# A fused two-block transformer kernel on one core: later slots for the layer work beside the expert gathers, another order of jobs in the tail

## The reference, cut to what matters

```python
# first block, its last part
ids, gates = top16 of two 128-way scores, per head     # 8 heads x 16 = 128 rows per token
ub = take(u_tab, ids); a = einsum('td,ted->te', h, ub)
w = gates * gelu(a)
vb = take(v_tab, ids); y = einsum('te,ted->td', w, vb)
x = rmsnorm(x + g2 * y, final_g)

# second block, two layers
for l in range(2):
    z = rmsnorm(x) @ w_in[l]         # g_q, g_k, g_v, g_lr, g_gate, c_q, c_kv, k_pe, m_gate
    o_gla = rms(gated_linear_attention(g_q, g_k, g_v, decay(g_lr))) * silu(g_gate)
    q, k, v = low-rank projections of rms(c_q), rms(c_kv), with head norms and rope
    o_mla = causal_softmax_attention(q, k, v) * silu(m_gate)
    x = x + concat(o_gla, o_mla) @ w_out[l]
```

## Time and profile before

| | us |
|---|---|
| median of three runs | 1138.64 |
| profiled execution | 1140.25 |
| its span | 1138.4 |
| PE / VectorE / ScalarE / GpSimd busy | 990.1 / 655.7 / 325.2 / 521.2 |
| chain that ended last: PE / DMA / GpSimd | 51% / 23% / 9% |

### The profile page before, as it was taken

The page is one execution under the profiler, slowest core; times in us unless marked ns, Lnnn a source line. Parts: engine busy times, 40 slices in busy tenths (PEclk is TensorE's granted clock), DMA queues, the critical chain, the costliest instruction groups (busy, mean ns, idle before and its releaser), DMA issues.

```text
span 1138.4 us, 11282 instructions
## 1 busy us (share of the span) xinstructions
PE 990.1 (87%) x3307; PEld 535.2 (47%) x3307; DVE 655.7 (58%) x1543; ACT 325.2 (29%) x813; POOL 521.2 (46%) x575
## 2 busy tenths in 40 slices
PE   3999999999997868878679899879889987987986
PEld 3868656855452323323235344335345333643653
DVE  5866776985755756856574774566554544142132
ACT  4123232222212111110144543233623211440441
POOL 1210011767777777777566456655554760000000
PEclk9999999999999998989989999999998988998999
DMA  9998955999999999999999999999997999548440
GB/s 341 321 391 308 337 205 170 385 376 408 409 410 412 410 413 413 411 412 402 408 410 409 406 410 399 406 405 409 408 410 279 400 409 389 212 162 282 162 148 19
DMA packets 142041, 394.92 MB, mean 347 GB/s; under 512 B 16744, under 2 KB 23456, under 8 KB 141856
## 3 DMA queue, kind: packets, MB, share of 16 engines
q0 software_dynamic: 75392, 274.86, 61.5%
q1 hardware_dynamic: 64224, 118.61, 28.7%
q10 hardware_dynamic: 2368, 0.76, 0.3%
HBM read 393.15 MB, written 1.05 MB: 346 GB/s over the span
## 4 chain that ended last, share of the span: by engine, by line
PE 51%; DMA 23%; POOL 9%; issue 7%; DVE 5%; ACT 4%; POOLq 0%; DVEq 0%; SPq 0%; ACTq 0%
PE bank L1720 16%; DMA wring<-in_peer_u,ids 14%; PE bank L1768 11%; PE bank L1454 8%; POOL wring L979 5%; DMA R<-in_w_in 3%; DMA wring<-in_peer_v,ids 3%; PE bank L1789 3%; PE bank L1531 2%; PE bank L1444 2%; DMA R<-in_peer_u,ids 2%; POOL R L979 2%; DVE R L1991 1%; DVE wring L2332 1%; ACT R L1292 1%
## 5 line engine op out<-in xcount | busy, mean ns | idle before, releaser
L2332 DVE CUSTOM_DVE_ANT_0 wring<-wring,bank 128x1024 f32<-128x1024 f32 x224 | 272.8, 1219 | 206.7 <-DMA wring<-in_peer_u,ids 203.4
L979 POOL DMA_INDIRECT wring<-in_peer_v,ids x224 | 214.1, 956 | 168.3 <-PE bank L1720 98.3
L1720 PE MATMUL bank<-wring,R 128*128 128x512 f32 x496 | 239.4, 628 | 32.8 <-ACT R L1218 23.1
L979 POOL DMA_INDIRECT wring<-in_peer_u,ids x224 | 211.4, 944 | 76.0 <-issue 56.4
L1720 PE MATMUL bank<-wring,modb 128*128 128x512 f32 x384 | 184.6, 621 | 25.1 <-ACT modb L1218 17.8
L1720 PEld LDWEIGHTS bank<-wring,R 128*128 128x128 f32 x496 | 95.9, 200 | 161.2 <-issue 130.1
L1720 PEld LDWEIGHTS bank<-wring,modb 128*128 128x128 f32 x384 | 72.2, 197 | 114.3 <-issue 95.9
L1018 POOL TENSOR_SCALAR small<-small 128x1 f32<-128x1 f32 (+3 forms) x15 | 2.9, 192 | 254.2 <-ACTq L1299 144.9
L1768 PE MATMUL bank<-R,hT 128*128 128x512 f32 (+1 forms) x192 | 94.5, 623 | 13.5 <-issue 6.8
L1768 PE MATMUL bank<-wring,hT 128*128 128x512 f32 (+1 forms) x192 | 88.6, 613 | 4.3 <-ACT hT L1399 2.7
L1454 PE MATMUL bank<-hT,wring 128*128 128x256 f32 x304 | 70.9, 392 | 1.8 <-DVE hT L2015 1.0
(11 more groups left out here) (374 smaller groups left out, 1248.7 us busy)
## 6 DMA issues: line engine op xcount, KB each, us to landing
wring<-in_w_in SPq DMA_DIRECT2D x14, 2048.0 KB, 14.5
wring<-in_ada_w SPq DMA_DIRECT2D x8, 2048.0 KB, 13.9
R<-in_w_in SPq DMA_DIRECT2D x8, 2048.0 KB, 21.1
wring<-in_w_out SPq DMA_DIRECT2D x6, 2048.0 KB, 10.8
wring<-in_ada_w SPq DMA_DIRECT2D x8, 1024.0 KB, 15.3
R<-in_w_out SPq DMA_DIRECT2D x4, 2048.0 KB, 20.3
wring<-in_peer_wq SPq DMA_DIRECT2D x2, 2048.0 KB, 10.2
wring<-in_peer_u,ids POOLq DMA_INDIRECT x224, 12.1
```

What stands on the lines that cost most here:

```text
L979: pool.indirect_dma_start(dst, None, table, bass.IndirectOffsetOnAxis(index, 0)).then_inc(landed, 16)
L1720: last = pe.matmul(pb[half][:, :], diag[b][:, s, :], v_place(n, b, s)[:, half * 512:(half + 1) * 512], start=False, stop=last_row, skip_gr ...
L2332: dve.tensor_tensor_reduce(row, row, h_psum(t), 1.0, 0.0, ALU.mult, ALU.add, a8[:, b, s:s + 1]).then_inc(u_free, 1)
```

## The change

`VISIT` goes from 52 to 59, so that visit 1 starts at slot 75 and not 68, and the last job in the shadow lies in slot 126, not 112. Within a visit, most jobs that read another engine's result move to one or two slots behind it. The three orders in the tail change: two of the eight pieces of `y2` of visit 1 and one `y2e` move to the beginning of visit 3; `mg` 0 and 1 move ahead of `qkt`, and `gge` behind `qkte`; `ms` 1, `mPT`, `go` and `gosq` move forward, `mPT` 2 and 3 with their evacuation go ahead of `goe`. SyncE starts chunk 6 of layer 1 four products earlier, and stores tile 0 of the output at the very end of its list.

```diff
-VISIT = 52
+VISIT = 59
@@ visit_slots
-    at(13, ("gqk", 2))
-    at(14, ("gqk", 3))
-    at(15, ("gqke",), ("gl",))
-    at(16, ("gate",), ("u", 0))
...
-    at(18, ("decays",), ("u", 1))
-    at(20, ("gv", 0), ("glaq",))
...
-    at(28, ("gg", 3), ("qkt",))
-    at(29, ("gge",), ("qkte",), ("go",))
-    at(30, ("mg", 0), ("gosq",))
...
+    at(14, ("gqk", 3))
+    at(15, ("cT",))
+    at(16, ("cTe",), ("gqke",))
+    at(17, ("gl",))
+    at(18, ("gate",), ("u", 0))
+    at(20, ("u", 1))
+    at(21, ("decays",), ("ue", 1), ("gv", 0))
...
+    at(25, ("gve",), ("gg", 0), ("keT",))
+    at(26, ("keR",), ("rope", 2), ("gg", 1), ("A",))
+    at(28, ("Am",), ("gg", 3), ("U",))
+    at(29, ("gge",), ("st",))
+    at(30, ("qkt",))
+    at(31, ("qkte",))
+    at(32, ("go",), ("mg", 0))
...
+    at(58, ("y2e", 1))
@@ tail_schedule
-    out = [("y2", 1, ch, p) for ch in range(2) for p in range(4)]
+    out = [("y2", 1, 0, p) for p in range(4)] + [("y2", 1, 1, p) for p in range(2)]
...
-        to(("xsq",), ("rms", 0), ("norm",), ("zT",), ("zTe",))
-        if v == LAYERS:
-            out.extend(("y2e", 1, ch) for ch in range(2))
+        to(("xsq",), ("rms", 0), ("norm",))
+        if v > LAYERS:
+            out += [("y2", 1, 1, p) for p in range(2, 4)]
+        to(("zT",), ("zTe",))
+        out.append(("y2e", 1, v - LAYERS))
...
-        to(*[("gg", p) for p in range(4)], ("gge",), ("keT",), ("keR",), ("A",), ("Am",), ("qkt",), ("qkte",))
-        to(("mg", 0), ("mg", 1), ("ms", 0), ("mk", 0), ("mk", 1), ("mx", 0), ("mx", 1), ("U",), ("st",))
-        to(("mPT", 0), ("mPTe", 0), ("mPT", 1), ("mPTe", 1), ("ms", 1), ("mk", 2), ("mk", 3), ("mx", 2), ("mx", 3))
-        to(("mg", 2), ("mPV", 0), ("mPV", 1), ("go",), ("gosq",), ("rms", 3), ("goe",), ("mPT", 2), ("mPTe", 2), ("mPT", 3), ("mPTe", 3))
-        to(("mg", 3), ("mge",), ("mPV", 2), ("mPV", 3), ("moe",), ("cT2", 0), ("cT2e", 0))
+        to(*[("gg", p) for p in range(4)], ("mg", 0), ("keT",), ("keR",), ("A",), ("Am",), ("mg", 1), ("qkt",), ("qkte",), ("gge",))
+        to(("U",), ("st",), ("ms", 0), ("mk", 0), ("mk", 1), ("mx", 0), ("mx", 1), ("ms", 1), ("mk", 2), ("mg", 2), ("mk", 3))
+        to(("mPT", 0), ("mPTe", 0), ("mPT", 1), ("mPTe", 1), ("mx", 2), ("mx", 3), ("go",), ("gosq",), ("rms", 3))
+        to(("mPV", 0), ("mPV", 1), ("mg", 3), ("mge",), ("mPT", 2), ("mPTe", 2), ("mPT", 3), ("mPTe", 3), ("goe",))
+        to(("mPV", 2), ("mPV", 3), ("moe",), ("cT2", 0), ("cT2e", 0))
@@ SyncE
-            sp.wait_ge(u_free, NG * GROUP)
-            for n in (6, 7):
...
+            sp.wait_ge(u_free, NG * GROUP - 4)
+            left_open(6)
+            sp.wait_ge(u_free, NG * GROUP)
+            left_open(7)
...
-                    sp.wait_ge(x_ready, X_BEFORE[2] + 1)
-                    sp.dma_start(out[0, 0:P, :], xrow[:, 0, :]).then_inc(out_done, 16)
...
+            sp.wait_ge(x_ready, X_BEFORE[3] + 1)
+            sp.dma_start(out[0, 0:P, :], xrow[:, 0, :]).then_inc(out_done, 16)
```

More of the change, by code:

```diff
@@ L208, in visit_slots @@
     at(0, ("xsq",))
-    at(2, ("norm",))
-    at(3, ("zT",), ("zTe",))
+    at(3, ("norm",))
+    at(5, ("zT",))
+    at(6, ("zTe",))
     for p in range(4):
[L212 to L216, removed]
-    at(13, ("gqk", 2))
-    at(14, ("gqk", 3))
-    at(15, ("gqke",), ("gl",))
-    at(16, ("gate",), ("u", 0))
-    at(17, ("gated",), ("ue", 0))
-    at(18, ("decays",), ("u", 1))
-    at(19, ("ue", 1))
@@ L224, in visit_slots @@
-    at(20, ("gv", 0), ("glaq",))
[L225 to L231, removed]
-    at(28, ("gg", 3), ("qkt",))
-    at(29, ("gge",), ("qkte",), ("go",))
-    at(30, ("mg", 0), ("gosq",))
-    at(31, ("mg", 1))
-    at(32, ("goe",), ("ms", 0))
-    at(33, ("mg", 2), ("mk", 0), ("mk", 1))
@@ L238, in visit_slots @@
[L238 to L255, removed]
+        at(7 + p, ("c", p))
+    at(11, ("ce",), ("gqk", 0))
+    at(12, ("gqk", 1))
+    at(13, ("cn",), ("gqk", 2))
+    at(14, ("gqk", 3))
+    at(15, ("cT",))
+    at(16, ("cTe",), ("gqke",))
+    at(17, ("gl",))
+    at(18, ("gate",), ("u", 0))
+    at(19, ("gated",), ("ue", 0))
+    at(20, ("u", 1))
+    at(21, ("decays",), ("ue", 1), ("gv", 0))
+    at(22, ("gv", 1))
@@ new lines, in visit_slots @@
+    at(23, ("glaq",), ("rope", 0), ("gv", 2))
+    at(24, ("rope", 1), ("gv", 3))
+    at(25, ("gve",), ("gg", 0), ("keT",))
+    at(26, ("keR",), ("rope", 2), ("gg", 1), ("A",))
+    at(27, ("rope", 3), ("gg", 2))
+    at(28, ("Am",), ("gg", 3), ("U",))
[3 more added lines that the diff above has]
+    at(32, ("go",), ("mg", 0))
+    at(33, ("gosq",), ("mg", 1))
+    at(34, ("mg", 2))
+    at(35, ("goe",), ("mg", 3))
+    at(36, ("ms", 0), ("mge",))
+    at(37, ("mk", 0), ("mk", 1))
@@ new lines, in visit_slots @@
+    at(38, ("mx", 0), ("mx", 1), ("ms", 1))
+    at(39, ("mPT", 0))
+    at(40, ("mPTe", 0), ("mk", 2), ("mk", 3), ("mPT", 1))
+    at(41, ("mPTe", 1), ("mx", 2), ("mx", 3))
+    at(42, ("mPV", 0), ("cT2", 0))
+    at(43, ("cT2e", 0), ("mPV", 1), ("mPT", 2))
+    at(44, ("mPTe", 2), ("mPT", 3))
+    at(45, ("mPTe", 3), ("y2", 0, 0))
+    at(46, ("mPV", 2))
+    at(47, ("mPV", 3))
+    at(48, ("moe",), ("y2", 0, 1))
+    at(50, ("cT2", 1))
+    at(51, ("cT2e", 1))
+    at(52, ("y2", 0, 2))
+    at(53, ("y2", 0, 3))
@@ L256, in visit_slots @@
+    at(54, ("y2e", 0), ("y2", 1, 0))
+    at(55, ("y2", 1, 1))
+    at(56, ("y2", 1, 2))
+    at(57, ("y2", 1, 3))
+    at(58, ("y2e", 1))
     return out
@@ L824, in program @@
         ROWS_BEFORE = [8 + 2 * v for v in range(NT * LAYERS)]
-        X_BEFORE = [NT + 2, NT + 3, NT + 5, NT + 7]
+        X_BEFORE = [NT + 2, NT + 3, NT + 5, NT + 6]
         def rms_known(eng, v, k):
@@ L917, in _, with left_open @@
             next_gains(1)
-            sp.wait_ge(u_free, NG * GROUP)
-            for n in (6, 7):
+            def left_open(n):
                 place = shadow_place(n, 1)[0]
                 layer_chunk(n, 1, shadow_ring[place], shadow_landed[place])
+            sp.wait_ge(u_free, NG * GROUP - 4)
+            left_open(6)
+            sp.wait_ge(u_free, NG * GROUP)
+            left_open(7)
             for n in (1, 0):
@@ L940, in _ @@
                         layer_chunk(n, 1, wring[:, n, :], w_landed[n])
+            sp.wait_ge(x_ready, X_BEFORE[3] + 1)
+            sp.dma_start(out[0, 0:P, :], xrow[:, 0, :]).then_inc(out_done, 16)
             sp.wait_ge(last_half_left, 1)
             sp.dma_start(out[0, P:S, 0:512], xrow[:, 1, 0:512]).then_inc(out_done, 16)
-            sp.wait_ge(x_ready, X_BEFORE[3] + 1)
+            sp.wait_ge(x_ready, X_BEFORE[3] + 2)
             sp.dma_start(out[0, P:S, 512:1024], xrow[:, 1, 512:1024]).then_inc(out_done, 16)
```

## The result

| | before | after |
|---|---|---|
| median | 1138.57 (4 runs) | 1124.83 (4 runs) |
| profiled execution, its span | 1140.25, 1138.4 | 1126.51, 1124.6 |
| PE / VectorE / ScalarE / GpSimd busy | 990.1 / 655.7 / 325.2 / 521.2 | 988.2 / 655.2 / 325.7 / 523.8 |

The ratio of after to before is 0.9882, 95% interval 0.9860 to 0.9904: 13.7 us faster, inside the range, where the forecast was 24.6. The work is the same. A line of before has a number about 12 higher in after (L1720 is L1732, L1768 is L1780, L2606 is L2618; SyncE's are 7 higher).

The account below looks back on a forecast made before the run. DMA bytes were taken to bound tile 1's expert rows, PE's gaps to matter in the tail. Terms -8.0 + 1.3 - 7.7 - 7.7 - 2.5 = -24.6 us took the median from 1138.64 to 1114.0, range 1107 to 1127.

Parts of the forecast that it names:

- The walk of the tail's order: PE followed job by job from `gg` to `y2` in visit 3: `y2` at 1112.0 against 1119.74; visit 2 likewise.
- the signs named ahead: No shadow stretch below 400 GB/s; chunk 6 10 us ahead of the last product; 23 us from `gg` to `y2`.
- The shadow, -8.0: Expert rows beside visits 0 and 1: new slots remove a hole of 9.1 us DMA time; ends -9.1 and 0.
- The seam, +1.3: Last gathers to `zT` of visit 2: early chunk 6 delays gathers, idle PE loses clock; ends -2.5 and +2.6.
- the 3.8 us: Seam: gathers running at 73% throughout beside chunk 6 end 3.8 us later, `norm` at 964.9.
- The clock's price of 2.6: Seam: after about 8 us of idle PE, `zT` and `c` run slow, 2.6 us lost.
- Visit 2, -7.7: Tail: `gg` to `y2` 23.1 us instead of 28.7, first `y2` 7.13 instead of 9.25; bounds -4 and -8.5.
- The start of visit 3, -2.5: Held `y2` pieces fill the gap before `zT`, so `zT` and `c` run at full clock; other end 0.
- Visit 3, -7.7: Tail: the new order brings `y2` to 1112.0 against 1119.74; bounds -8.5 and -4.
- The rings run dry elsewhere: Rival, shadow: PE late just before a group at another place, nothing won there; 1122, chance 0.20.
- The slower case: Shadow: `gg` 0's chunk takes 29.1 us, PE waits 14, a hole of 11 us per visit; 1145, chance 0.04.
- The tail gives half: Rival, tail: ScalarE or a bank holds `mx` or `go`, `goe` 4 us later in each visit; 1122, chance 0.14.

Follow-up runs that it names:

- old seam: Changed kernel with all eight pieces of `y2` of visit 1 in front and chunk 6 started behind the last product; 1125.22, ratio 0.9870.
- the kernel with the narrow part last: Changed kernel (chunk 6 early) with chunk 1's 64 KB load issued behind its large one; 1125.21, ratio 0.9887.
- the first experiment: Kernel before with only the tail's new order, old slots, eight `y2` pieces in front and chunk 6 late; 1124.36, ratio 0.9862.

## Why the prediction was right and where it was wrong

The time lies 2 us inside the upper end of the range, 1127, and nearer to the 1122 of each single rival than to 1114.0. The walk of the tail's order held in both visits, for its own reasons. Shadow, seam and the start of visit 3 together gave some 9 us less than forecast, and only the width of the range covered that.

Of the signs named ahead, the tail's came (23.0 us, no gap of 4 us), and so did chunk 6, 13.6 us ahead of its old place, and the gap of 8.18. Two went against the prediction: the windows were to stay above 400 GB/s and the DMA share was not to fall anywhere in the shadow, and 890 to 900 us has 324 and 0.97. (The 410 GB/s "in every window but three" of before was too even a reading: the share was at its ceiling there, the rates were 381 to 415.)

**The shadow, -8.0: the mechanism held in part, the term was mis-sized.** The hole went, and `gg` 0's chunk cost PE 2.5 us at most. The last product came 3.9 us earlier, not 8 (935.97 against a mean of 932.1 with the new slots and a late chunk). The step that failed is that the bytes were counted, and a stall of 9.1 us was taken to be a loss of 9.1. One part is the gains: in before they were started at 878.0, at the end of the hole, and the 30 us behind 880 lost 0.7 us of DMA time; in after those lost 2.8 (372 of 411 GB/s). The runs without the gains there put the last product at 927.6 to 929.2, 7.8 before 935.97. That looks like the forecast, but about 2.4 of it are the gains' own bytes, which before had to move as well. That the hole had sheltered the gains in before is argued; no run took them out of that kernel. The other part is that the hole of the one profiled execution was the largest of three seen, so the median could not gain what that execution lost: the new slots alone gave 2.1. What made the hole, and so whether `go` did, stays open.

**The seam, +1.3: the step that failed is the 3.8 us.** By the share of 27% the last gathers would be 3.8 later, and they are 6.2; the share itself fits (the two chunks of `w_out` take 18.5 us to land in after, of which 5.1 are 28%). The sum let the gathers be issued as before and only move more slowly. But the issue of a v gather hangs on the product eight rows earlier, and that on a v row of the same slowed stream: PE's waits of 1.34 and 2.10 us are that loop, and GpSimd's of 2.38 and 3.15 behind it. The later the last gathers are, the more of chunks 7 and 1, which are started with the last u product (933.8), shares the rings with them, which fits the landing of 13.2 for 11.1. That the early chunk is the cause has been tried; the loop as its way is read from these waits, and the share of chunks 7 and 1 is argued. The 5.1 us worked out there from the Trainium skill (DMA: Bandwidth & Descriptors, Queues, rings and completion order) come nearer to the 6.2 but by the same wrong step. The clock's price of 2.6 was right in kind: 0.9 at `zT` and 1.6 to 2.7 at `c`. With 10.2 us earlier forecast and 13.6 had, the chunk was also more in the way. Without this one edit the kernel takes 1117.1 and not 1124.8. The term's own ends were -2.5 and +2.6; with the cold `c` it came to +4.6 here (0.7 at the end of `c` and the 3.9 that the shadow had won), outside both. In the medians it is hidden: with the old seam the kernel takes 1125.2 and with the new one 1124.8, since the held pieces give what the early chunk costs.

**Visit 2, -7.7:** right to the tenth (23.0 us from `gg` to `y2`, first `y2` 7.13). The 7.13 was luck, though: of the ten kernels with this order, seven had it at 8.8 to 10.1. It went with a cold `c` in the next term.

**The start of visit 3, -2.5:** measured -0.8 in after, and 13.0 us for 15.5, which is -2.5, in the three executions where `c` was warm. The step read a low clock as the effect of the long gap before `zT`; with only the short gaps of 1.25 and 0.78 left, it came too, in the two executions whose `y2` ahead had been warm. The two terms have to be taken together: -8.5 in after and in the kernel with the narrow part last, where -10.2 was forecast.

**Visit 3, -7.7:** 23.0 us from `gg` to `y2` as walked; the first `y2` at 8.83 for 7.13 took 1.7 back. In before it was warm behind the gap of 4.18, so the term had nothing to win from the clock there and could only lose.

**The rivals.** "The rings run dry elsewhere" had the right total for the shadow (nothing won, 1122) by the wrong cause. The slower case was far: PE's longest wait on `in_w_in` in the shadow was 2.5 us, not 14. "The tail gives half" fell with the first experiment.

## What to carry to other kernels

Before a load is started earlier beside gathers that fill the rings, follow the loop: who issues the next gather, and whether that waits on a row of the same stream; 2 MB started 10 us early cost 8 us here, more than its 5.1 us of bytes, and 2 to 5 where other work filled the wait. Try two edits at one seam apart as well as together. A stall that is filled is worth its length less what used it and is pushed into full rings, and its length should be read from more than one execution. What the clock gives after a short gap is to be put into the range, not into the sum.

## What the runs showed of the hardware

- **TensorE's clock behind a short gap can go either way, and two pieces are not independent.** The same instructions with the same gaps of 1.25 and 0.78 us had `c` at 8.15 (granted clock 0.79 over the piece) or 6.46 (1.00), cold where the `y2` before it was warm; `y2` behind gaps of 1.58 and 0.69 us took 7.13 or 8.6 to 10.1. In after the granted clock was 0.95 over the whole span in one execution and 0.96 in the others, whose spans were 1.3 to 2.9 us shorter.
- **Gains loaded to every partition (1920 numbers to each of 128, in rows of 0.5 to 4 KB, 1.0 MB) cost the stream of gathers 3.9 us** in the end of the last product (932.1 against a mean of 928.2 without them). By an estimate 2.4 of it are the bytes at 411 GB/s; the rest goes with the rate of the stretch from 880 to 910 us, 341 to 372 GB/s with them and 387 to 401 without.
- **The same loads behind chunks 7, 1 and 0 landed late though the engines were not full:** the eighth, of 16 KB, 11.6 us after it was started (952.5 and 964.1), with 264 GB/s in the window from 950 to 960 and 71 from 958 to 961.
